# Three of four early rows of a gather weighed on PE by diagonal matrices in the gate spread

## The reference

```python
def block(args):
    h_blk, e_blk, g_blk = args
    u = u_emb[e_blk]
    a = jnp.einsum('bthkd,btd->bthk', u, h_blk).astype(jnp.float32)
    act = (jax.nn.gelu(a) * g_blk).astype(h_blk.dtype)
    return jnp.einsum('bthk,bthkd->btd', act, v_emb[e_blk])
```

## Time and profile before

| | us |
|---|---|
| median of 3 runs | 4034.56 (4030.64 to 4038.61) |
| profiled execution | 4050.63 |
| its span, first to last instruction | 4048.8 |

### The profile page before, as it was taken

How to read it: one execution, slowest core, us unless ns; L and a number is a source line. 1 busy time by engine, 2 the same in 40 slices (tenths; PEclk the granted TensorE clock), 3 DMA queues, 4 the chain that set the end, 5 groups by cost and what they waited for, 6 DMA issues and landing times. The chain is left out here.

```text
span 4048.8 us, 46819 instructions
## 1 busy us (share of the span) xinstructions
PE 3394.2 (84%) x15298; PEld 2673.5 (66%) x15298; DVE 3201.9 (79%) x5528; ACT 1457.9 (36%) x2400; POOL 1888.9 (47%) x1508
## 2 busy tenths in 40 slices
PE   6999999998899998868989989897333788898886
PEld 5766676766577886646777777775333567677664
DVE  5677776777753513699999999998999798898988
ACT  3465555656542433222322322322222222222222
POOL 2433444333222131345556665554555466666664
PEclk9999999998999999979999999998555799999998
DMA  2111111111343322479999999997988999999997
GB/s 85 47 49 51 53 37 53 44 51 53 121 181 125 120 73 95 156 248 353 357 353 354 370 357 354 344 362 289 362 323 334 332 392 396 396 399 397 395 383 283
DMA packets 300338, 964.44 MB, mean 238 GB/s; under 512 B 30656, under 2 KB 63680, under 8 KB 297024
## 3 DMA queue, kind: packets, MB, share of 16 engines
q0 software_dynamic: 147456, 536.94, 35.3%
q1 hardware_dynamic: 150336, 390.95, 26.6%
q10 hardware_dynamic: 2304, 33.56, 2.1%
HBM read 861.18 MB, written 100.14 MB: 237 GB/s over the span
## 5 line engine op out<-in xcount | busy, mean ns | idle before, releaser
L2446 POOL DMA_INDIRECT spread_vrow<-in_v_rows,shared_pick_rows x512 | 712.5, 1392 | 464.9 <-DVE spread_y L2474 339.8
L1582 POOL DMA_INDIRECT ret_urow<-in_u_rows,shared_pick_rows x512 | 630.0, 1230 | 493.0 <-DVE ret_urow L2193 358.5
L2474 DVE SCALAR_TENSOR_TENSOR spread_y<-spread_vrow,shared_pick_coef,spread_y 128x1024 f32<-128x1024 f32 x512 | 639.3, 1279 | 10.1 <-DMA spread_vrow<-in_v_rows,shared_pick_rows 10.0
L2193 DVE SCALAR_TENSOR_TENSOR ret_urow<-ret_urow,ret_h_rows 128x1024 f32<-128x1024 f32 x512 | 609.8, 1227 | 28.7 <-DMA ret_urow<-in_u_rows,shared_pick_rows 26.5
L157 PE MATMUL shared_carry<-ret_hhi,shared_w_hi 128*128 128x512 f32 x1152 | 475.1, 412 | 108.6 <-DVE shared_w_lo L1382 66.1
L157 PE MATMUL spread_banks<-spread_ahi,spread_vhi 128*128 128x512 f32 x1024 | 418.8, 409 | 121.0 <-DVE spread_alo L2487 121.0
L157 PE MATMUL shared_carry<-shared_wide_hi,shared_w_hi 128*128 128x512 f32 x1152 | 459.1, 399 | 28.9 <-DVE shared_wide_lo L585 11.2
L158 PE MATMUL shared_carry<-ret_hlo,shared_w_hi 128*128 128x512 f32 x1152 | 466.0, 405 | 0.0
L158 PE MATMUL shared_carry<-shared_wide_lo,shared_w_hi 128*128 128x512 f32 x1152 | 454.8, 395 | 0.0
L159 PE MATMUL shared_carry<-shared_wide_hi,shared_w_lo 128*128 128x512 f32 x1152 | 454.2, 394 | 0.0
L158 PE MATMUL spread_banks<-spread_alo,spread_vhi 128*128 128x512 f32 x1024 | 412.1, 402 | 0.0
(11 more groups left out here) (295 smaller groups left out, 6764.6 us busy)
## 6 DMA issues: line engine op xcount, KB each, us to landing
spread_vraw<-in_peer_v SPq DMA_DIRECT2D x128, 512.0 KB, 13.8
shared_w_raw<-in_peer_u SPq DMA_DIRECT2D x65, 512.0 KB, 7.1
gelu_u<-shared_front SPq DMA_DIRECT2D x128, 256.0 KB, 8.3
gates<-spread_stage ACTq DMA_DIRECT2D x16, 2048.0 KB, 9.6
spread_act<-gelu_u SPq DMA_DIRECT2D x128, 256.0 KB, 11.9
spread_graw<-gates SPq DMA_DIRECT2D x16, 2048.0 KB, 23.3
ret_wraw<-in_peer_u SPq DMA_DIRECT2D x63, 512.0 KB, 7.2
shared_w_raw<-in_w_mix SPq DMA_DIRECT2D x56, 512.0 KB, 3.4
```

The costliest lines, as they stand in the source:

```text
L1582: nc.gpsimd.indirect_dma_start(slots[s][:], None, u_rows, bass.IndirectOffsetOnAxis(tables.rows[:, t, hd * K + j:hd * K + j + 1], 0)).then ...
L2193: nc.vector.scalar_tensor_tensor(out=slots[s][:], in0=slots[s][:], scalar=1.0, in1=h_rows[:, t], op0=ALU.mult, op1=ALU.mult, accum_out=tab ...
L2446: nc.gpsimd.indirect_dma_start(v_slots[s][:], None, v_rows, bass.IndirectOffsetOnAxis(tables.rows[:, t, j:j + 1], 0)).then_inc(row_loaded[ ...
L2474: nc.vector.scalar_tensor_tensor(out=y[:, t], in0=v_slots[s][:], scalar=tables.coef[:, t, j:j + 1], in1=y[:, t], op0=ALU.mult, op1=ALU.add ...
```

## The change

In each step of the gate spread the first BY_PE = 3 of the four picks go to PE. For each, ACT makes a diagonal matrix `diag` [128 x 128] f32 of the pick's 128 coefficients, by scaling an identity per partition (six such buffers), and PE multiplies it by the row slot in two f32 matmuls of 512 columns, adding up in the four PSUM banks that the gate spread leaves free (`y_sums`, two tiles of y by two halves). These 96 picks belong to tiles 0 and 1; the fourth pick of a step stays on DVE and belongs to tile 2 or 3. PE's three come after its gate matmuls of the step. After the loop and the first products of the body DVE adds the two sums to `y[:, 0]` and `y[:, 1]`; PE's first use of those banks in the body waits for that.

The gate spread has 11 row slots in place of 7; the four more lie where the second gate buffer is loaded later, and that load now also waits until they are free. The body keeps seven slots. After the first 128 picks the tile of a pick is that with the fewest picks so far (and not the one just taken), so tiles 2 and 3 come first until all have 48. POOL makes the identity before the first fetch. A fetch waits for the last user of its slot, on PE (`weighed`) or on DVE (`picked`). At the end ACT's square of tile t waits for the last pick of that tile, or of the slot into which the square goes, in place of the last of all.

```diff
--- before.py
+++ after.py
@@ -2320,7 +2320,7 @@
         NG = KEYS // E
         NQ = 4
         QC = NC // NQ
-        SV = 7
+        SV, SV_FIRST = 7, 11
         G8 = 2 * E
         PICKS = GT * PH * TOPK
         EARLY = 4
@@ -2339,10 +2339,13 @@
         vhi = m.at("vhi", [P, NQ, E, QC * P], F32R, at(84))
         vlo = m.at("vlo", [P, NQ, E, QC * P], F32R, at(100))
         y = m.at("y", [P, GT, D], F32, at(116))
-        v_slots = [m.at(f"vrow{s}", [P, D], F32, at(132 + 4 * s)) for s in range(SV)]
+        v_slots = [m.at(f"vrow{s}", [P, D], F32, at(132 + 4 * s)) for s in range(SV_FIRST)]
         iota = m.at("iota", [P, KEYS], F16, at(186))
         ones = m.at("ones", [P, P], F32, at(187))
         g_sb = m.at("gain", [P, NC], F32, at(188))
+        DIAGS = 6
+        diag = [m.at(f"diag{i}", [P, P], F32, at(184) + 512 * i) for i in range(4)] + [m.at(f"diag{4 + i}", [P, P], F32, at(189) + 512 * i) for i in range(2)]
+        ident = m.at("ident", [P, P], F32, at(186) + 512)
         y_sq = m.at("y_sq", [P, GT], F32, at(188) + 64)
         y_norm = Rsqrt(m, "y_norm", GT, [m.at(f"y_{what}", [P, GT], F32, at(188) + 96 + 32 * i)[:]
                                          for i, what in enumerate(("mean", "inv", "rstd"))])
@@ -2350,6 +2353,7 @@
         norm = Rsqrt(m, "norm", TD, [graw[0][:].rearrange("p n e t -> p (n e t)")[:, TD * i:TD * i + TD] for i in range(3)])
         banks = m.ps("banks", [P, 8, H])
         ps = banks[:, 0:NB].rearrange("p b (x k) -> p b x k", k=KEYS)
+        y_sums = banks[:, NB:NB + 4].rearrange("p (t h) n -> p t (h n)", h=2)
 
         made, one1_made, eq_made, gated = m.sem("made"), m.sem("one1_made"), m.sem("eq_made"), m.sem("gated")
         g_done, staged = m.sem("g_done"), m.sem("staged")
@@ -2365,13 +2369,35 @@
         sum_done, sum_read = m.sem("sum_done"), m.sem("sum_read")
         y_made, out_stored = m.sem("y_made"), m.sem("out_stored")
         slot_held = m.sem("slot_held")
-        row_loaded = [m.sem(f"row_loaded{s}") for s in range(SV)]
-        picked = m.sem("picked", start=SV + GT)
+        row_loaded = [m.sem(f"row_loaded{s}") for s in range(SV_FIRST)]
+        picked, weighed = m.sem("picked"), m.sem("weighed")
+        diag_made, y_joined, ident_made = m.sem("diag_made"), m.sem("y_joined"), m.sem("ident_made")
         y_loaded, y_squared, y_read = m.sem("y_loaded"), m.sem("y_squared"), m.sem("y_read")
         y_scaled, y_stored = m.sem("y_scaled"), m.sem("y_stored")
         block = m.block()
 
         FIRST_PICKS = EARLY * N
+        BY_PE = 3
+        order, made_of = [], [0] * GT
+        for d in range(PICKS):
+            if d < FIRST_PICKS:
+                n, i = divmod(d, EARLY)
+                t = (BY_PE * n + i) % 2 if i < BY_PE else 2 + n % 2
+            else:
+                t = min((t for t in range(GT) if t != order[-1][0]), key=lambda t: made_of[t])
+            order.append((t, made_of[t]))
+            made_of[t] += 1
+        by_pe = [d < FIRST_PICKS and d % EARLY < BY_PE for d in range(PICKS)]
+        upto = {kind: [sum(p is kind for p in by_pe[:d]) for d in range(PICKS + 1)] for kind in (True, False)}
+        PE_PICKS = upto[True][PICKS]
+        slot_of = [d % SV_FIRST if d < FIRST_PICKS else (d - FIRST_PICKS) % SV for d in range(PICKS)]
+        latest_first = {slot_of[d]: d for d in range(FIRST_PICKS)}
+        held_by, landed, latest = [], [], {}
+        for d in range(PICKS):
+            held_by.append(latest.get(slot_of[d], (None, 0))[0])
+            landed.append(16 * (latest.get(slot_of[d], (None, 0))[1] + 1))
+            latest[slot_of[d]] = d, landed[d] // 16
+        before = [max([x for x in range(d) if order[x][0] == order[d][0] and by_pe[x] is by_pe[d]], default=None) for d in range(PICKS)]
 
         def picks_of(g, place, places):
 
@@ -2388,6 +2414,10 @@
             def load_gates(i):
                 if i >= 2:
                     sync.wait_ge(weighted, G8 * (i - 1))
+                if i == 1:
+                    last = [latest_first[s] for s in range(SV, SV_FIRST)]
+                    sync.wait_ge(weighed, max(upto[True][d + 1] for d in last))
+                    sync.wait_ge(picked, max(upto[False][d + 1] for d in last))
                 sync.dma_start(graw[i % 2][:].rearrange("p n e t -> p n (e t)"),
                                g_out[:, :, G8 * i:G8 * i + G8, :].rearrange("n p j t -> p n (j t)")).then_inc(g_loaded[i % 2], 16)
 
@@ -2439,10 +2469,16 @@
                            allow_small_or_imprecise_dtypes=True).then_inc(made, 1)
             nc.gpsimd.memset(ones[:], 1.0).then_inc(made, 1)
 
+            pool.wait_ge(made, 2)
+            nc.gpsimd.affine_select(out=ident[:], in_=ones[:], pattern=[[-1, P]], compare_op=ALU.is_equal, fill=0.0,
+                                    base=0, channel_multiplier=1).then_inc(ident_made, 1)
+
             def fetch(d):
-                s, t, j = d % SV, d % GT, d // GT
-                pool.wait_ge(picked, d + GT + 1)
-                pool.sem_inc(slot_held, 1)
+                s, (t, j) = slot_of[d], order[d]
+                last = held_by[d]
+                if last is not None:
+                    pool.wait_ge(weighed if by_pe[last] else picked, upto[by_pe[last]][last + 1])
+                    pool.sem_inc(slot_held, 1)
                 nc.gpsimd.indirect_dma_start(v_slots[s][:], None, v_rows, bass.IndirectOffsetOnAxis(tables.rows[:, t, j:j + 1], 0)
                                              ).then_inc(row_loaded[s], 16)
 
@@ -2468,9 +2504,14 @@
             def weigh_picks(d0, d1):
 
                 for d in range(d0, d1):
-                    s, t, j = d % SV, d % GT, d // GT
-                    dve.wait_ge(row_loaded[s], d // SV * 16 + 16)
-                    dve.wait_ge(picked, d + SV + 1)
+                    if by_pe[d]:
+                        continue
+                    s, (t, j) = slot_of[d], order[d]
+                    dve.wait_ge(row_loaded[s], landed[d])
+                    if before[d] is not None:
+                        dve.wait_ge(picked, upto[False][before[d] + 1])
+                    elif t < 2:
+                        dve.wait_ge(y_joined, t + 1)
                     nc.vector.scalar_tensor_tensor(out=y[:, t], in0=v_slots[s][:], scalar=tables.coef[:, t, j:j + 1],
                                                    in1=y[:, t], op0=ALU.mult, op1=ALU.add).then_inc(picked, 1)
 
@@ -2511,6 +2552,9 @@
             for e in range(E):
                 weigh(0, e)
                 split(0, e)
+            dve.wait_ge(weighed, PE_PICKS)
+            for t in range(2):
+                tt(y[:, t], y[:, t], y_sums[:, t], ALU.add).then_inc(y_joined, 1)
 
             PLACES = 16
 
@@ -2581,10 +2625,21 @@
                         for i in range(2):
                             mm = nc.tensor.matmul(ps[:, bank, x], one1[:, b, t], gate[b][:, i, t], start=(i == 0), stop=(i == 1))
                     mm.then_inc(g_done, 1)
+                for d in range(EARLY * n, EARLY * n + BY_PE):
+                    s, (t, j) = slot_of[d], order[d]
+                    last = d + 2 >= FIRST_PICKS - EARLY + BY_PE
+                    pe.wait_ge(row_loaded[s], landed[d])
+                    pe.wait_ge(diag_made, upto[True][d + 1])
+                    for h in range(2):
+                        mm = nc.tensor.matmul(y_sums[:, t, h * H:h * H + H], diag[upto[True][d] % DIAGS][:], v_slots[s][:, h * H:h * H + H],
+                                              start=(j == 0), stop=last)
+                    mm.then_inc(weighed, 1)
             pe.wait_ge(staged, N * NB)
             for g in range(NG):
                 for k in range(NC):
                     q, dp = k // QC, slice(k % QC * P, k % QC * P + P)
+                    if g == 0 and k in (4, 6):
+                        pe.wait_ge(y_joined, k // 2 - 1)
                     if k % QC == 0:
                         pe.wait_ge(vlo_made, g * NQ + (q + 1))
                     for e in range(E):
@@ -2618,6 +2673,13 @@
                     act_eng.wait_ge(stored[slot], 16 * (quarter // SLOTS))
                 if n < NQ:
                     values(0, n)
+                for d in range(EARLY * n, EARLY * n + BY_PE):
+                    x, (t, j) = upto[True][d], order[d]
+                    if x == 0:
+                        act_eng.wait_ge(ident_made, 1)
+                    if x >= DIAGS:
+                        act_eng.wait_ge(weighed, x - DIAGS + 1)
+                    nc.scalar.activation(diag[x % DIAGS][:], ident[:], ACT.Copy, scale=tables.coef[:, t, j:j + 1]).then_inc(diag_made, 1)
                 for bank in range(NB):
                     act_eng.wait_ge(g_done, n * NB + bank + 1)
                     t = n % 2 * B + 4 * bank
@@ -2644,7 +2706,7 @@
                 nc.scalar.activation(square_of[:, k % 2] if k else total_of, acc[:, k], ACT.Square).then_inc(squared, 1)
 
             for t in range(GT):
-                act_eng.wait_ge(picked, SV + GT + PICKS)
```

(1 more changed line is left out.)

## The result

The changed kernel takes **3972.5 us** in the median (3970.02 to 3974.44, 4 runs) against 4036.59 us for the kernel before beside it: ratio 0.9842, 95% interval 0.9825 to 0.9859, 64 us faster. The forecast was 4001.5 with a range from 3987 to 4027.

The account below looks back on a forecast made before the run. DVE was taken to bound the gate spread, DMA bytes after the change. Terms −31.6 − 3.0 (first steps) + 0.4 + 1.5 + 2.5 − 3.1 = −33.3 us; 33 off the median 4034.56 gave 4001.5 us, range 3987 to 4027.

Parts of the forecast that it names:

- DVE gives the bound to DMA: Gate spread: DVE bounds the 9.57 us step; after losing three picks (3.65 us), DMA bounds it, a shrink of 1.17 us.
- The step of 8.4 us: Gate spread: DMA moves 3.15 MB per step at 378 GB/s; 27 steps gain 31.6 us.
- PE's sums: Gate spread: PE's gate matmuls (2.3 us) and f32 row matmuls (5.3 us) take 7.6 us a step at 2.4 GHz.
- Rival 2: Gate spread: PE stays at 1.2 GHz, step 13.8 us, kernel slower at about 4159 us; chance 0.09.
- rival 1: Gate spread: PE or POOL becomes the bound, step 8.8 to 9.3 us, kernel 4013 to 4027 us; chance 0.15.
- Slots: Gate spread: eleven row slots are 23 us of rows, a row waits at worst a step, some 14 us left for flight.
- POOL: Gate spread: POOL's four row issues take 6.3 us a step, bounds 5.0 and 9.1, hidden under 8.
- rival 3: Gate spread: POOL is shut out during DVE's f16 products, step 9.8 us, kernel about 4040 us; chance 0.04.
- The edges: Around the gate spread and at the tail: identity +0.4, last store +1.5, join +2.5, squares of y −3.1 us.
- the squares: Tail: with ACT's wait per tile, three of four squares of y run beside the last picks, −3.1 us.
- The join's 2.5: Before the body: DVE's two 128x1024 additions of PE's sums from PSUM, charged whole at +2.5 us, bounds 0 and 3.
- Rival 4: Where last store, gate load and prefetched rows meet: the stage's gain is given back, kernel 4026 to 4034 us; chance 0.06.

## Why the prediction was wrong

**DVE gives the bound to DMA: right.** Two picks on PE, half of PE's work, and half of the store show it from three sides.

**The step of 8.4 us: wrong, and this is the step that failed.** It was 3.15 MB over 378 GB/s, and 378 was 336/0.89, a rate divided by a share as though the share grew in step with the bytes. The half store run shows that it doesn't (0.98 at 374 GB/s). The second witness, the body's 395 GB/s, was taken for a ceiling because its share was 1.02; the third, 360 GB/s for the last store and the gate load, was a mix with 1 KB pieces, which went at 347 GB/s by themselves. With 409 GB/s, the loads' own flat rate, the sum is 3.146/0.409 = 7.69 us. That this is the measured step to the digit is luck: the views count some 1% of other bytes beside the 3.146 MB, and the same stage took up to 7.89 us in other profiles. The trace of before held the number. Its rate in 40 slices of 6.5 us, from 2880 to 3140 us:

```profile
GB/s 380 351 403 388 391 257 384 374 226 383 384 211 388 388 208 405 372 218 404 352 233 399 350 238 396 362 226 388 377 225 394 379 203 401 352 282 372 367 234 381
```

Between the gaps that DVE left, single slices reach 403 to 405; a mean over several slices mixes the gaps in. The range inherited the fault: its low end took 395 GB/s as the best case (8.0 us), so 27 x 0.3 us, the first steps and the edges lay outside. The page of the Trainium skill that the prediction cites for 358 GB/s a core ("DMA: Bandwidth & Descriptors") has, under Measured, 425 GB/s for 16 MB on a single core. This case is nearer to that one: it held 409 and 413 GB/s for 170 us and more.

**PE's sums: right.** The gate matmuls took 1.95 us at the high clock (bounds 1.8 to 3.6, taken 2.3), twelve f32 records 5.37 us with the last one's end (5.3 forecast), one step 7.1 us of busy time (7.6). The clock rose as forecast: 32 gate matmuls in 3.60 us at 2816.13, in 1.95 or 1.96 from the third step on wherever all 32 are recorded, and 0.99 was granted from step 4 to 31. Rival 2, and rival 1, whose 8.8 to 9.3 us lay on the wrong side, fall.

**Slots: too light.** The prediction said "Eleven slots are 23 us of rows at that pace" and that some 14 us are left for flight. That eleven were enough was partly luck: at the step that came, a slot's turn was 21.1 us, with 11.6 of it in flight; nine slots already cost 0.69 us a step, and with seven the whole gain is gone. This line carried the forecast and had no price in it.

**POOL: right.** It was busy 126.49 us in 27 steps, 4.7 us a step and some 1 us of pauses, never the bound. About three in ten of its issues there took 1.6 to 1.97 us, so long ones are common, but the mean is 1.2 us, where the sign of rival 3 was over 1.8 each. Rival 3 falls: DVE's f16 products fill 4.9 of 7.69 us, and four issues, 4.7 us, would not fit into the 2.8 us left.

**The edges: small errors on both sides.** The identity cost 0.1 in place of 0.4, the last store 0.1 for 1.5, the squares −3.0 for −3.1. The join's 2.5 is not to be seen, but lies within the scatter of the body, so whether the body absorbs it stays open. Rival 4 (the gain given back at the joint) falls: 24.2 us for 24.1.

## What to carry to other kernels

When an engine's work is taken away, the gain is the distance to the next bound, so that bound deserves the care: take a DMA ceiling from slices of some us between the gaps, not from a mean over gaps or a mean divided by its share. Where a slot is filled by DMA and freed by an engine that itself waits for another's product, count the loop from fetch to fetch through all of them; here four slots decided between 64 us and nothing. Compare traces from a mark at the changed phase, as unchanged code ahead of it moved by 18 us between two profiles.

## What the runs showed of the hardware

In this kernel loads in 4 KB pieces held 409 GB/s on one core, rows beside 2 MB stores 403 to 415 in six profiles, and a load in 1 KB pieces, nearly alone, 347. The DMA share in the records is no measure of what is left: 0.98 at 374 GB/s, 1.03 at 408, and 1.03 at 395 to 397 in the body. Plain f32 matmuls of 128x512 with a diagonal stationary operand took 0.43 us per record at the high clock, the dense ones of the earlier trace rows 0.44, so the zeros save nothing. With these matmuls PE's clock was granted at 0.99 over 208 us, though PE waited there 16.2 us in 13 pieces, the longest 3.8 us. Where it waited longer in its gate spread the mean clock was lower: 0.93 with 52.4 us of waits (seven slots), 0.88 with 64.4 (half of PE's columns).
